# First adaLN modulation in four channel blocks by narrow TensorE products, with four weight tiles run as the channels come, and two joined pool steps

## The reference

```
ada = (silu(c) @ w_ada[l] + b_ada[l]).reshape(9, 1024)
u = rmsnorm(x, norm_g[l, 0]) * (1 + ada[1]) + ada[0]
x = x + 0.5 * ada[2] * swiglu(u, w_ff1_up[l], w_ff1_down[l])          # 1024 -> 2 x 2816 -> 1024
u = rmsnorm(x, norm_g[l, 1]) * (1 + ada[4]) + ada[3]
x = x + ada[5] * mix(u)     # windowed attention and causal multi-scale pooling, gated, merged, projected
u = rmsnorm(x, norm_g[l, 2]) * (1 + ada[7]) + ada[6]
x = x + 0.5 * ada[8] * swiglu(u, w_ff2_up[l], w_ff2_down[l])
```

## Time and profile before

| | us |
|---|---|
| median of three runs | 2094.58 |
| lowest, highest | 2093.84, 2095.78 |
| the profiled execution | 2098.55 |
| its span, first to last instruction | 2096.7 |
| PE busy in it | 2071.8 (99%) |
| DVE, POOL, ACT busy | 931.9, 686.2, 544.5 |
| mean granted clock of TensorE | 0.988 of 2.4 GHz |

### The profile page before, as it was taken

One profiled execution on the slowest core, in us unless ns is written; L12 is line 12 of the kernel. 1 busy time (PEld: TensorE's weight loads), 2 busy tenths in 40 slices (PEclk: granted clock), 3 DMA queues, 4 the chain that ended last, 5 costly groups with the idle time before them and its releaser, 6 DMA issues.

```text
span 2096.7 us, 24621 instructions
## 1 busy us (share of the span) xinstructions
PE 2071.8 (99%) x10190; PEld 1753.5 (84%) x10190; DVE 931.9 (44%) x1433; ACT 544.5 (26%) x802; POOL 686.2 (33%) x272
## 2 busy tenths in 40 slices
PE   7999999999999999999999999999999999999999
PEld 6888888897888988888898888889878888888888
DVE  6543144567546644311254433347665665221121
ACT  2322122231522422122232211223233233221220
POOL 0344434412000244534425453443100004453451
PEclk6999999999999999999999999999999999999999
DMA  8365556622223366433326754654221435332331
GB/s 286 97 184 179 148 151 180 176 62 61 71 80 112 110 186 190 126 101 108 122 72 168 204 160 112 195 160 100 72 80 61 124 118 146 93 103 81 101 103 68
DMA packets 323069, 264.82 MB, mean 126 GB/s; under 512 B 25014, under 2 KB 302862, under 8 KB 322958
## 3 DMA queue, kind: packets, MB, share of 16 engines
q1 hardware_dynamic: 321280, 262.70, 42.4%
q10 hardware_dynamic: 1678, 0.55, 0.1%
HBM read 261.12 MB, written 2.10 MB: 126 GB/s over the span
## 4 chain that ended last, share of the span: by engine, by line
PE 97%; DVE 1%; DMA 1%; issue 0%; ACTq 0%; ACT 0%; SPq 0%; DVEq 0%
PE bank L1213 27%; PE bank L1215 27%; PE bank L1214 27%; PE bank L1289 2%; PE bank L1290 2%; PE bank L1293 2%; PE ps L1307 1%; PE ps L1478 1%; PE bank L1240 1%; PE bank L1242 1%; PE bank L1241 1%; PE ps L1406 1%; PE ps L1388 1%; DMA ada_first<-in_w_ada 0%; PE ps L1364 0%; PE ps L1371 0%
## 5 line engine op out<-in xcount | busy, mean ns | idle before, releaser
L530 POOL TENSOR_TENSOR w_lo<-stage,w_hi 128x1024 fp32r<-128x1024 f32 (+1 forms) x239 | 660.6, 2784 | 1219.2 <-ACT w_hi L578 1172.3
L1213 PE MATMUL bank<-u_hi,w_hi 128*128 128x512 f32 x1776 | 702.4, 395 | 0.0
L1215 PE MATMUL bank<-u_hi,w_lo 128*128 128x512 f32 x1776 | 693.1, 390 | 0.0
L1214 PE MATMUL bank<-u_lo,w_hi 128*128 128x512 f32 x1776 | 692.8, 390 | 0.0
L578 ACT ACTIVATE w_hi<-stage 128x1024 fp32r<-128x1024 f32 (+2 forms) x337 | 349.3, 1073 | 716.5 <-DMA stage<-in_w_ff_up 365.2
L1213 PEld LDWEIGHTS bank<-u_hi,w_hi 128*128 128x128 f32 x1776 | 334.4, 188 | 70.4 <-issue 2.4
L1215 PEld LDWEIGHTS bank<-u_hi,w_lo 128*128 128x128 f32 x1776 | 334.1, 188 | 70.5
L1214 PEld LDWEIGHTS bank<-u_lo,w_hi 128*128 128x128 f32 x1776 | 334.5, 188 | 69.5 <-issue 2.4
L900 DVE TENSOR_TENSOR prod<-silu,bank 128x512 f32<-128x512 f32 x88 | 60.5, 688 | 557.3 <-PE bank L1215 537.2
L1213 PE MATMUL bank<-h_hi,w_hi 128*128 128x512 f32 x744 | 290.0, 390 | 0.0
L1215 PE MATMUL bank<-h_hi,w_lo 128*128 128x512 f32 x744 | 289.7, 389 | 0.0
(11 more groups left out here) (149 smaller groups left out, 1546.2 us busy)
## 6 DMA issues: line engine op xcount, KB each, us to landing
stage<-in_w_ff_up SPq DMA_DIRECT2D x176, 512.0 KB
ada_stage<-in_w_ada SPq DMA_DIRECT2D x128, 512.0 KB, 3.8
stage<-in_w_ff_down SPq DMA_DIRECT2D x32, 1408.0 KB
stage<-in_w_in SPq DMA_DIRECT2D x18, 1024.0 KB
ada_first<-in_w_ada SPq DMA_DIRECT2D x16, 512.0 KB, 11.9
stage<-in_w_out SPq DMA_DIRECT2D x8, 1024.0 KB
stage<-in_w_in SPq DMA_DIRECT2D x16, 256.0 KB
stage<-in_w_in SPq DMA_DIRECT2D x8, 512.0 KB
```

Of the source, the lines that this page charges most:

```text
L530: nc.gpsimd.tensor_tensor(stage_tile(w_lo, kind, n), t, hi_tile(n, depth(kind, n)), ALU.subtract).then_inc(lo_ready, 1)
L1213: mm(bank[n % BANKS][:, :], hi[:, k, :], rhs_hi(k), start=(k == 0), stop=False)
L1214: mm(bank[n % BANKS][:, :], hi[:, k, :], rhs_lo(k), start=False, stop=False)
L1215: last = mm(bank[n % BANKS][:, :], lo[:, k, :], rhs_hi(k), start=False, stop=(k == k_n - 1))
```

## The change

- **DMA order.** Eight `ada_block` tiles, 128 x 8 x 256, hold the first two vectors' weights, a shift and a scale tile for each of four channel blocks of 256. SP issues x, block 0, the weight loads of tiles 0 to 3, block 1, block 2, the load of tiles 4 and 5, block 3, without a wait. c comes by its own small DMA first on ACT's queue, with the constant matrix.
- **x and the statistics.** x is turned by 128 frames at a time, DVE and ACT copy half each. ACT squares all channels of 128 frames at once, DVE reduces them over the channel groups.
- **The modulation.** `block_sums` makes both vectors of a block by products whose weights are `c_act` widened to 32 columns and whose moving operand is the weight block itself. Four such products write the four quarters of the PSUM partitions. DVE copies, PE turns the rows back, DVE makes `shift_b` and `scale` for two channel groups.
- **Four tiles.** `block_tiles` runs tiles 0 to 3 over the two channel groups of a block, with 512 columns. The low parts of tiles 0 to 2 are made by DVE, of tile 3 by POOL.
- **The later groups.** `ada_reduce` sums `ada_acc` by four narrow products of 256 columns with a `pick` matrix, which puts group g in row g of each quarter; one or more groups later `ada_turn` turns the rows back with two transposes. `ADA_STEP` is 3 instead of 4.
- **Pool stage.** ACT copies the four tiles to `pool_in` and makes the high part with the scale; DVE makes the low part from PSUM in one step. `neg_sink` moves to the mixing part.

```diff
+            def block_sums(b):
+                pe.wait_ge(block_in[b], 32)
+                if b >= 2:
+                    pe.wait_ge(block_kept, b - 1)
+                dst = (ps7, bank[4])[b % 2]
+                for k in range(KT):
+                    for j in range(4):
+                        v, half = divmod(j, 2)
+                        last = mm(dst[32 * j:32 * j + 32, 0:P], c_act[:, k:k + 1].to_broadcast([P, 32]),
+                                  ada_block[2 * b + v][:, k, half * P:(half + 1) * P], start=(k == 0), stop=(k == KT - 1))
+                last.then_inc(block_done, 1)
+
+            def block_turn(b):
+                pe.wait_ge(block_kept, b + 1)
+                if b:
+                    pe.wait_ge(first_vec, 2 * b - 1)
+                nc.tensor.transpose(ps5[:, 0:P], block_rows[b % 2][:, :], ident).then_inc(block_turned, 1)
+
+            def block_tiles(b):
+                pairs = (2 * b, 2 * b + 1)
+                for k in pairs:
+                    pe.wait_ge(u_hi_ready, 2 * k + 2)
+                    if b == 0:
+                        pe.wait_ge(u_lo_ready, 2 * k + 2)
+                    for n in range(START_TILES):
+                        hi, lo = hi_tile(n, KT), stage_tile(w_lo, "ff", n)
+                        if b == 0 and k == 0:
+                            pe.wait_ge(hi_ready, n + 1)
+                        mm(bank[n][:, :], hi[:, k, :], u_hi[:, k, :], start=(k == 0), stop=False)
+                        if b == 0:
+                            mm(bank[n][:, :], hi[:, k, :], u_lo[:, k, :], start=False, stop=False)
+                        else:
+                            mm(bank[n][:, :], lo[:, k, :], u_hi[:, k, :], start=False, stop=False)
+                    if b:
+                        pe.wait_ge(u_lo_ready, 2 * k + 2)
+                        for n in range(START_TILES):
+                            last = mm(bank[n][:, :], hi_tile(n, KT)[:, k, :], u_lo[:, k, :], start=False, stop=(k == KT - 1))
+                            if k == KT - 1:
+                                last.then_inc(tile_done, 1)
+                if b == 0:
+                    for n in range(START_TILES):
+                        pe.wait_ge(lo_ready, n + 1)
+                        for k in pairs:
+                            mm(bank[n][:, :], stage_tile(w_lo, "ff", n)[:, k, :], u_hi[:, k, :], start=False, stop=False)
+
             pe.sem_inc(tile_done, BANKS)
+            pe.wait_ge(c_in, 32)
+            nc.tensor.transpose(ps5[:, 0:KT], c_rows[:, :], ident[0:KT, 0:KT]).then_inc(c_turned, 1)
+            turn_x(0)
+            turn_x(1)
             pe.wait_ge(consts_in, N_CONSTS)
...
+            turn_x(2)
+            turn_x(3)
             pe.wait_ge(act_step, 1)
-            for k in range(KT):
-                pe.wait_ge(ada_first_in[2 * k], 16)
-                for m in range(KT):
-                    mm(ps7[:, m:m + 1], ada_first[2 * k][:, m * P:(m + 1) * P], c_act[:, k:k + 1],
-                       start=(k == 0 and m == 0), stop=(k == KT - 1), skip_group_check=True)
...
+            for h in range(2):
+                pe.wait_ge(x_summed, 2 * h + 2)
+                for j in (2 * h, 2 * h + 1):
+                    last = mm(ps5[:, j:j + 1], sq_sum[:, j * P:(j + 1) * P], ones[:, :], start=True, stop=True)
+                last.then_inc(norm_summed, 1)
...
+            block_sums(0)
+            block_turn(0)
+            block_tiles(0)
+            block_sums(1)
+            block_turn(1)
+            for b in range(1, BLOCKS - 1):
+                block_sums(b + 1)
+                block_turn(b + 1)
+                block_tiles(b)
+            block_tiles(BLOCKS - 1)
```

DVE at the start, ACT's first rounding, and `ada_reduce`:

```diff
+            for j in range(JT):
+                dve.wait_ge(turned, 2 * j + 1)
+                nc.vector.tensor_copy(x_t[:, 0:4, j * P:(j + 1) * P],
+                                      bank[2 * j % 4][:, :].rearrange("p (m f) -> p m f", f=P)).then_inc(x_kept, 1)
+                if j:
+                    sum_squares(j - 1)
+            sum_squares(JT - 1)
+            for h in range(2):
+                stats(0, 0, h)
+            for b in range(BLOCKS):
+                block_vectors(b)
+                block_u(b)
+                if b == 0:
+                    for n in range(AHEAD):
+                        low_part("ff", 0, n)
+                if b in (1, 2):
+                    for step in range(4 * (b - 1), 4 * b):
+                        angle_step(step)
...
-                    if tiles + n + AHEAD < DEPTH * TILES:
+                    if START_TILES <= tiles + n + AHEAD < DEPTH * TILES:
                         round_weights("ff", tiles, loads, n + AHEAD)
...
-                for m in range(KT):
-                    last = mm(ps7[:, m:m + 1], ada_acc[:, m * P:(m + 1) * P], ones[:, :], start=True, stop=True)
+                for j in range(4):
+                    last = mm(ps7[32 * j:32 * j + 32, 0:ADA_Q], pick[:, g - groups[0], :],
+                              ada_acc[:, j * ADA_Q:(j + 1) * ADA_Q], start=(g == groups[0]), stop=(g == groups[-1]))
```

More of the change, by code:

```diff
@@ L102 @@
 ADA_GROUPS = 3 * FF_GROUPS
-ADA_STEP = 4
+ADA_STEP = 3
+ADA_Q = D // 4
 REDUCE_STEPS = {ADA_STEP + (g + 1) * KT: g for g in range(FF_GROUPS)}
+TURN_STEPS = [ADA_STEP + (g + 1) * KT + 1 for g in range(FF_GROUPS)]
 NEWTON = 12
-VEC_STEPS = 2 + 3 * 2
+VEC_STEPS = 1 + 3 * 2
 FH = S // 2
@@ L358, in pieces_before, with turn_sets, turns_before @@
             return l * ADA_PIECES + (0, 2 * FF_ADA, 2 * FF_ADA)[i] + half * FF_ADA
+        def turn_sets(l, i, half):
+            if half:
+                return [range(FF_GROUPS)] if i == 0 else []
+            return [range(1), range(1, FF_GROUPS)] if i == 0 or l < DEPTH - 1 else [range(1)]
+        def turns_before(l, i, half=0):
+            return 5 * l + (0, 3, 3)[i] + 2 * half
         def ff_pieces(l, i, half):
@@ L691, in _, with first_weights @@
                                       ).then_inc(late_in, 16)
[L692 to L699 removed]
+            def first_weights(n):
                 s, count, _ = slot_of("ff", n)
@@ L910, in ff_half @@
                         close_first(l, i)
-                    if n in REDUCE_STEPS and REDUCE_STEPS[n] * KT < ff_pieces(l, i, half):
-                        ada_group(l, i, half, REDUCE_STEPS[n])
+                    for t, groups in enumerate(turn_sets(l, i, half)):
+                        if n == TURN_STEPS[groups[-1]] - 1:
+                            keep_rows(l, i, half, groups[-1])
+                        if n == TURN_STEPS[groups[-1]]:
+                            ada_vectors(l, i, half, t, groups)
                     if n == 18 and half == 0:
@@ new lines, in _ @@
+            dve.wait_ge(setup_step, DEPTH)
+            nc.vector.tensor_copy(lay[:, :], vec[:, 0, :]).then_inc(vec_step, 1)
+            for j in range(JT):
+                dve.wait_ge(turned, 2 * j + 1)
[6 more added lines that the diff above has]
+                stats(0, 0, h)
@@ L1328, in one @@
                         ada_reduce(l, i, half, REDUCE_STEPS[n])
+                    for t, groups in enumerate(turn_sets(l, i, half)):
+                        if n == TURN_STEPS[groups[-1]]:
+                            ada_turn(l, i, half, t)
                 if half > 0:
@@ L1332, in ff_half @@
                         one(n)
-                for n in range(FIRST, FF_TILES - 2 * half):
+                for n in range(FIRST if l or i or half else START_TILES, FF_TILES - 2 * half):
                     one(n)
```

396 lines of the change are left out of this document (236 added, 160 removed).

## The result

The changed kernel takes **2077.18 us** (median of four runs, 2076.52 to 2077.89), against 2094.21 for the kernel before on the same chip (2093.52 to 2095.78): a ratio of 0.9919 with a 95% interval of 0.9907 to 0.9931, 17.0 us less. The forecast was 2079. Its total came out within 2 us, but that was luck: two of its three terms were off by about 7 us, in opposite directions. Most of what follows is about that.

The account below looks back on a forecast made before the run. The prediction took PE, busy 99% of the span, as the bound. Start 5.5, groups 7.3 and pool stage 2.7 sum to 15.5 us gained, giving 2079 us on the median; range 2063 to 2104, its own case 2074 to 2086.

Parts of the forecast that it names:

- (a): Start, constants: they land at 11.0 us (10 to 14), and DVE waits for them ahead of its x copies.
- (d): Start, DMA: 6.3 MB take 22 us and all 13.6 MB 46 us, so the transfers are hidden.
- (b): Start, x copies and squares: DVE's reduction takes 1.1 us, each of four turns 2.0, last sum ends at 20.1.
- (c): Start, statistics: 24 steps take 4.7 us, to 24.8; after the spread, first narrow products start (S0) at 25.9.
- (e): Narrow products of a modulation block: records overlap in pairs across quarters, 3.4 us a block; serial 6.8, four abreast 1.7.
- The second rival: Four abreast: quarters fully overlap, 1.7 us a block, 31.1 us gained, 2063.5 us; chance 17%.
- (f): Start, block 0: sums 6.8 us at half clock, low parts follow, PE ends block 0 at 43.3, idle some 6 us.
- (g): Start, blocks 1 to 3: block 2's turn waits on DVE until 53.0, tiles(1) ends at 58.5, all four tiles at 73.4.
- (h): Before tile 4: PE newly waits 3.6 us for its low part; tile 4 starts at 77.0, 5.5 us earlier.
- the fourth rival: Group reductions pay for changing between narrow and full products, 5 to 11 us in all; 2084 to 2090 us; chance 7%.
- serial: First rival: quarters don't overlap, 6.8 us a block; 2100 to 2105 us, middle 2102; chance 28%.
- The clock's case: Third rival: narrow products keep the clock low; 2093 us in pairs, 2125 with serial products; chance 10%.

Follow-up runs that it names:

- the other set's run of after: The changed kernel run again unedited, as standard beside experiments on another chip: 2076.91 us, ratio 0.9915 to the kernel before.
- a0_after: Another profiled run of the unedited changed kernel; PE waited 3.73 us for block 2's rows, with the grant staying at 1.00 behind it.

## Why the prediction came out as it did

The sum was 15.5; 17.0 was measured between the medians. By parts, from the runs (the groups' and the pool stage's from the kernels without them, the start's from the kernel with it alone):

| | predicted | measured |
|---|---|---|
| start | 5.5 | -1.4 (start alone against before, within its interval of no change) |
| groups | 7.3 | 14.9 |
| pool stage | 2.7 | 3.6 |
| sum | 15.5 | 17.1 |

**(a), (d): right.** The constants' rows are turned at 10.61 (taken 11.0), without a wait of PE. No product of the start waited for a block or a weight tile by DMA.

**(b), (c): the reduction was mis-sized, and a term was left out.** The reduction takes 1.90 us instead of 1.1, above the upper end of 1.4. It was bounded by reductions and sums of other shapes, not by one that reads 1024 elements across the channel groups. With it the last sum ends at 22.05 instead of 20.1. Between it and the statistics PE still has to sum over the partitions; (c) had nothing for that, and it takes 1.1. So the statistics begin at 23.15, their steps take 4.6 (4.7 forecast), and S0 is at 28.93, 3.0 us late.

**(e): the step that failed.** "Records are served in order, the two records of a matmul use the same quarter and so follow one another, and the second overlaps the first of the next quarter" gave 3.4 us a block; it is 1.95. What failed is the first half of the sentence: the two records of a product do not follow one another. Four records of four products start within 0.02 us, and their second records 0.109 us later, so a block is 16 steps of 0.109 and not 32. With most products in one quarter it is 6.52, with the quarters one after another 5.95, where at each change four records of the next quarter start beside the last four of the old one. These three show that a record waits for its own quarter, and that with the quarters in turn it never holds up a neighbour. I had drawn from the order of starts in the rows that the two records of one product must follow one another in full; nothing in a row said so. The Trainium skill (TensorE: Matmul & The Clock Gate, Part 3: Packing small matmuls) gives 2.38 for three column groups; here four give 6.52 / 1.95 = 3.3 by the time of a block, and the full 4 by the distances between starts (four records every 0.109 us instead of one). The Trainium skill's factor of up to 4 (TensorEngine Tiling (Array Packing), Theoretical Speedup) agrees with that. The strict order of matmuls that the prediction set beside it does not hold product by product: the second record of a product starts behind the first records of the products that follow it, and what order the records had in PE's queue isn't shown. The second rival's price for (e) was the right one.

**(f): right by two errors, which is luck.** Tiles(0) ended at 43.4 against 43.3: 3.0 late at S0, made up in the sums (3.53 instead of 6.8, at the slow pace). Behind the sums the path was as forecast: DVE's three low parts end at 40.20 (40.4), POOL's fourth at 42.68 (43.0; with two products of 0.227 behind it, that makes 43.5 and not the 43.3 of the forecast). PE was idle for 3.4 us there and not 6, since its own products ran at half pace to 38.9.

**(g): mechanism right.** The turn of block 2 does wait for DVE behind the angle steps, at 51.71 (53.0 forecast). DVE of after, in order of time (the first of four angle steps, and the copy that PE waits for):

```profile
49.59 0.42 DVE L1205 CAST angle<-pos_i 128x512 f32<-128x512 int32 x1
...
51.37 0.28 DVE L1231 COPY block_rows<-ps 128x128 f32<-128x128 f32 x1
```

Missing was the clock: in this run tiles(1) ran 3.3 us at 0.5, which costs 1.6 and takes back more than the 1.3 by which DVE was early (59.0 against 58.5). Most of those 1.3 are block 1's sums, which were 1.4 shorter and let DVE begin earlier; block 2's, as much shorter, didn't help, since DVE was the later one there.

**(h): right, again without the clock.** PE waits 3.48 us for POOL's low part (3.6 forecast, where its own 4.2 less 0.7 make 3.5) and starts tile 4 at 76.15 (77.0). Behind it 3.3 us at half clock take back 1.7 in this run; in the two others it was some 6 us at half clock. Undoing both waits gave 8.8 us (7.6 by the other set's run of after), more than the 5.3 of the waits themselves (3.48, and 3.74 less 1.95). The half clock behind tile 4's wait went with it; the one behind block 2's did not. How much of the difference is the clock isn't measured, since the falls vary between runs of one kernel.

**The start's gain was then lost behind it**, which no step had: 2.4 to 4.6 at tile 5 in the three profiled runs of after, 2.7 at tile 5 and at the first group with the start alone, and by the end nothing that can be measured, 2.9 of it in three waits of about 1 us for DVE steps held by POOL. The prediction took everything behind tile 4 as a shift without consequence.

**Groups:** that quarters overlap was right, and the size hung on (e). A group costs 0.77 where pairs would have been 1.07 and a quarter of the serial time 0.5. The Trainium skill's drain on a change of mode (TensorEngine Tiling (Array Packing), Key Properties) can be at most what eight quarters of 0.213 (0.43) leave of the 0.77, 0.34 for both changes of form together, so it doesn't undo the gain; the fourth rival falls. A turn costs 0.23 (0.31).

**Pool:** right. Both waits are gone (2.7 of the 3.6) and nothing took their place; ACT had the time.

**The two runs' difference.** The prediction set off the 4 us by which the profiled run of before lies above its median. The trace of before shows them, in PE in order of time, where a group waits:

```profile
1794.58 2.41 PE L1307 MATMUL ps<-ones,ada_acc 128*128 128x1 f32 x16 [1.10 <-DVE ada_acc L881]
```

and the stretch behind it, with the columns of the stretches above:

```profile
1795.90:1802.70 6.80, 6.80 (x20) 5.55 (x20) 0.17 (x1) 0.10 (x1) 3.92 (x2) 0.50 0.00 0
```

The grant is 0.5 for 6.8 us; 1.1 and half of 6.8 make 4.5, near the 4.0 between the profiled run and the median. Forecasting on the median was right. Here a wait of only 1.1 us stands ahead of the half clock.

**Of the rivals,** serial is excluded by 1.95 a block. Four abreast was the true mechanism, but its time of 2063.5 wasn't reached: it took 12.0 for the start. The clock's case was wrong about the narrow products, which ran in stretches with a grant of 1.00 in blocks 1 to 3, and right that the clock costs something; it fell behind waits of PE. "Each us more a block costs some 4 at the start" was too steep for these kernels: 4.57 more a block cost 12.9, 2.8 each, partly because the longer sums of block 2 filled PE's wait for DVE there, 3.74 in after and 0.38 in the kernel with most products in one quarter.

## What to carry to other kernels

Narrow f32 products can be nearly four times as cheap if they write to four different quarters of the partitions and the quarters are issued in turn; with the loops the other way round most of it is lost. A wait of PE can cost more than its length, since a half clock may come behind it: 1.7 us more behind a wait of 3.48 here. But waits of this length had a price between nothing and some 3 us in the three profiled runs of the same kernel, and a wait cut from 3.7 to 1.95 us kept its half clock, so only the wait's own length can be counted on. Before counting a shift of the schedule as harmless, look at which DVE steps with operands in SBUF will stand beside POOL's long ones, because a step of 0.2 to 0.7 us can last as long as POOL's instruction.

## What the runs showed of the hardware that I had not expected

- 64 records of 128 columns in f32: 1.95 us with quarters in turn, 5.95 with the quarters one after another, 6.52 with 56 of them in one quarter. In turn, four records start within 0.02 us and the next four 0.109 us later; the two records of one product are never neighbours. With the quarters one after another, four records overlap at each change.
- The half clock behind a wait of PE at the same place: none in one and 3.3 us or more in two of the three profiled runs of the changed kernel, with the same wait of 3.7, and 3.3 us behind a wait of 1.95.
- A DVE step beside a POOL low part: 0.49 became 2.44 (TENSOR_SCALAR, 128x512), 0.43 became 3.34 (CAST), 0.69 became 3.58 (TENSOR_TENSOR), and a step on two columns took 1.75.
- The record of the granted clock can be wrong at the start. Block 0 of after, from 28.93, took 3.53 us at a granted clock that the record gives as 1.00, and the one-column records of the squares went at 0.213 with the record at 1.00. The stretch of after, and block 0 of `a0_after`, the same kernel (columns as above):

```profile
28.90:32.50 3.60, 3.56 (x65) 2.97 (x64) 0.00 (x0) 0.00 (x0) 0.00 (x0) 1.00 0.36 91
...
29.50:33.10 3.60, 3.60 (x65) 2.97 (x64) 0.00 (x0) 0.00 (x0) 0.00 (x0) 0.50 0.36 94
```

and one of the kernel in which PE sums the squares:

```profile
20.00:28.00 8.00, 8.00 (x39) 8.00 (x39) 0.00 (x0) 3.14 (x4) 0.00 (x0) 1.00 1.12 335
```

In all three, the distances between records say half pace, and in `a0_after`, where the block took 3.64 us, the record says so too. So it is the record of after that is wrong there, and at the start the distances are to be trusted.
